# A two-block transformer forward pass on one core: the feed-forward's gated products are turned by VectorE in 32x32 blocks, where TensorE transposed them

## The chip, the cores and the metric

The kernel runs on 1 core of one Trainium2 chip. The metric is the device time of one execution in microseconds; lower is better.

## The reference, cut to what matters

256 tokens, model width 1024, float32. The first block has two layers, each with a feed-forward, a mixer (a latent attention in the first layer, a forget-gate attention in the second), a second feed-forward and a gated embedding; a second block with a pooling branch and a dilated attention follows. There are four feed-forwards of this form, with D_FF = 2816:

```
def swiglu(x, w_in, w_out):
    gate, up = jnp.split(x @ w_in, 2, axis=-1)
    return (jax.nn.silu(gate) * up) @ w_out

h = h + FFN_HALF * swiglu(rms_norm(h, g_ffn1[i]), ffn1_w_in[i], ffn1_w_out[i])
```

## The kernel before, in words

Each engine has a hand-written program, and semaphores order them. Every float32 product is made of three products of rounded parts: a matrix is split into a high part (a rounded copy, float32r) and a low part (the remainder), and hi x hi, hi x lo and lo x hi are added up in PSUM.

**Weights.** They come in groups of 128 x 2048 values. A group has a slot in each of three rings of four: `raw` (filled by SP's DMA queue, two transfers), `wh` (ScalarE's rounded copy, `split` at L1455 to L1461) and `wl` (VectorE's difference, `split` at L1983 to L1988). ScalarE's split of group g waits until TensorE has used group g-4 (`w_used`), TensorE waits for VectorE's part (`lo_done`), and SP may load raw again when VectorE's part is done (`room`, L439).

**A feed-forward** (`ffn` in each engine's program; f0 to f3) has two phases, with 33 groups of weights in all.

In the first phase there are 11 chunks (FCH) of 256 columns of gate and 256 of up. Each takes two groups (k = 0, 1), and TensorE makes 24 products of 128 x 512 for each: `tall_group`, L614 to L616. The result, for two tiles of 128 tokens, lies in one of two accumulators, by turns. ScalarE makes silu of the gate half (`silus`, L1544, into `sg`), and VectorE multiplies it with the up half (`gated`, L2140, into `a_n`, tokens on partitions). The second phase needs these products with features on partitions. So TensorE transposes them: four transposes of 128 x 128 for each chunk into a PSUM bank `M[c % 2]` (`turn_products`, L768 to L778; every transpose of the kernel is recorded at L690). They are placed between the two groups of the next chunk. ScalarE rounds the bank into `ah` (`round_a`, L1550), and VectorE writes the remainder into `al` (`rest_a`, L2147).

In the second phase there are 11 groups of `w_out` (L647 to L651; the first by `wide_first`), one for each chunk: TensorE multiplies `ah` and `al` of chunk c with the group and adds up all eleven. The eleventh chunk is transposed after the first of these groups. Before each group TensorE waits for the chunk's remainder (`m_read`).

In both phases ScalarE and VectorE split one or two groups ahead of TensorE. Their order for a chunk is: split, round or remainder of the chunk before, split, silu or gated product. On TensorE, ScalarE, VectorE and SP the middle chunks are a loop (`Fori`), the first one or three written out.

In f0 TensorE also makes a small bias table in three parts (L814, at chunks 2, 4 and 6 of the second phase), and VectorE copies it to `tsb` (L2178) after all its remainders. ScalarE stores `tsb` with a DMA (L1586) after the next norm. In f1 and f3 a tile `p_n` is transposed after the first group of the second phase, rounded to `ph` and its remainder written to `pl`.

Of the kernel before, what the change touches and what calls it, by code (L numbers as in the profile page):

```python
# [18 lines left out]
F32 = mybir.dt.float32  # L19
# [7 lines left out]
P = 128  # L27
# [49 lines left out]
def plan():  # L77


    sizes = {  # L80
        "norm": (0, 0, (1, 1, 1, 1), (4, 4, 4, 4)),
        "ffn": (33, 13, (6, 5, 0, 0), (6, 5, 0, 0)),
        "ffn_t": (33, 13, (6, 5, 0, G3), (6, 5, 0, G3)),
        "ffn_p": (33, 13, (6, 5, 1, 0), (6, 5, 1, 0)),
        "mla": (14, 12 + H, (H // 2 + 2, H // 2 + 2, H + 2, H + 1), (H + 2, H + 2, H + 2, H + 1)),
        "fox": (17, 9, (H, H, H, H + 3), (H, H, H, H + 3)),
        "ple": (5, 4, (0, 0, 0, 0), (0, 0, 0, 0)),
        "b2": (40, 26, tuple([n + 2 * (b == 3) for b, n in enumerate(U_FILLS)]),
               tuple([n + 2 * (b == 3) for b, n in enumerate(U_FILLS)])),
    }  # L90
    order = [("n0", "norm"), ("f0", "ffn_t"), ("n1", "norm"), ("mla", "mla"), ("n2", "norm"),
             ("f1", "ffn_p"), ("n3", "norm"), ("p0", "ple"), ("n4", "norm"), ("f2", "ffn"), ("n5", "norm"),
             ("fox", "fox"), ("n6", "norm"), ("f3", "ffn_p"), ("n7", "norm"), ("p1", "ple"), ("n8", "norm"),
             ("b2", "b2")]
    g = q = 0
    f, r = [0] * 4, [0] * 4
    at = {}
    for name, kind in order:
        at[name] = (g, q, tuple(f), tuple(r))
        dg, dq, df, dr = sizes[kind]  # L100
        g, q = g + dg, q + dq
        f = [a + b for a, b in zip(f, df)]
        r = [a + b for a, b in zip(r, dr)]
    return at, g


PLAN, NGROUPS = plan()


def heads_at():  # L110
# [40 lines left out]
def build(nc, I, out):  # L151
    with ExitStack() as ctx:
# [58 lines left out]
        x = region()  # L211
        ah = x("ah", [P, 2 * FCH, S], F32R)
        al = x("al", [P, 2 * FCH, S], F32R)
        sg = x("sg", [P, 2, NT, 256])
        a_n = x("a_n", [P, 2, NT, 256])
        p_n = x("p_n", [P, NT, PLE])
        ph = x("ph", [P, 2, S], F32R)
        pl = x("pl", [P, 2, S], F32R)
# [15 lines left out]
        kpe = x("kpe", [P, NT, ROPE])  # L234
        kpr = x("kpr", [P, NT, ROPE])
        x = region()
        x("below", [P, 1], offset=2 * (2 * FCH * S * 4) + 2 * (2 * NT * 256 * 4) - 32)
        causal_f = x("causal_f", [P, P])
        onehot = x("onehot", [33, TAB])
        rb = x("rb", [33, NH2])  # L240
        tsb = x("tsb", [H8, TAB])
        hraw = x("hraw", [P, 4])
        rgain = x("rgain", [P, 2, ROPE])
        freq = x("freq", [P, 16])
# [97 lines left out]
        rstd_done = sem("rstd_done")  # L342
        xh_done = sem("xh_done")
        silu_done = sem("silu_done")
        ah_done = sem("ah_done")
        gate_done = sem("gate_done")
        lat_sq = sem("lat_sq")
        lat_rstd = sem("lat_rstd")
# [240 lines left out]
        def _(pe):  # L589
# [164 lines left out]
            def ffn(name, nname, r, after, r_after, with_p=None):  # L754
# [3 lines left out]
                def chunk(c, i=0):  # L758

                    q, g = q0 + c, g0 + 2 * c  # L760
                    open_acc(q, i)
                    for k in range(2):
                        wait_group(g + k, i)
                        tall_group(g + k, q, xh, xl, 4 * k, 4, 512, k == 0, k == 1)
                        if k == 0:
                            turn_products(c - 1, i)

                def turn_products(c, i=0):  # L768

                    b, q = c % 2, q0 + c  # L770
                    pe.wait_ge(acc_read[q % 2], acc_reads(q) + 2 * i)
                    if r0[b] + c // 2 > 0:
                        pe.wait_ge(m_read[b], r0[b] + c // 2 + i)
                    for t in range(NT):
                        for k in range(2):
                            mm = turn(b, slice(k * S + t * P, k * S + (t + 1) * P),
                                      a_n[:, b, t, k * P:(k + 1) * P])
                    mm.then_inc(m_ready[b], 1)  # L778

                peel = 3 if g0 == 0 else 1  # L780
                first_fill(nname, r, g0, q0)
# [5 lines left out]
                q, g = q0 + FCH, g0 + 2 * FCH  # L787
                for c in range(FCH):
                    wait_group(g + c)
                    pe.wait_ge(m_read[c % 2], r0[c % 2] + c // 2 + 1)  # L790
                    if c == 0:
                        wide_first(g, q, ah, al)
                    else:
# [1 line left out]
                            wide_tile(g + c, q, t, ah, al, 2 * c, False, c == FCH - 1,  # L795
                                      turn_h(after, r_after) if t and c == FCH - 1 else None)
                    if c == 0:
                        turn_products(FCH - 1)
                        if with_p is not None:
                            open_m(2, r0[2])  # L800
                            pe.wait_ge(p_in, 16 * (with_p + 1))
                            for t in range(NT):
                                for k in range(2):
                                    mm = turn(2, slice(k * S + t * P, k * S + (t + 1) * P),
                                              p_n[:, t, k * P:(k + 1) * P])
                            mm.then_inc(m_ready[2], 1)
# [632 lines left out]
        def _(act):  # L1439
# [95 lines left out]
            def ffn(name, r):  # L1535
# [11 lines left out]
                def round_a(c, i=0):  # L1547
                    b = c % 2
                    act.wait_ge(m_ready[b], f0[b] + c // 2 + 1 + i)
                    act.activation(ah[:, bass.ds(i * 4 + 2 * c, 2), :],  # L1550
                                   M[:, b, :].rearrange("p (k n) -> p k n", k=2), ACT.Copy).then_inc(ah_done, 1)

                peel = 3 if g0 == 0 else 1
                for c in range(peel):
                    split_to(g0 + 2 * c + 3)
                    if c:
                        round_a(c - 1)
                    split_to(g0 + 2 * c + 4)
                    silus(c)
                    if g0 == 0 and c == 1:  # L1560

                        act.wait_ge(angles, 1)
                        act.activation(cs[:, :, :, :], rc[:, :, :, :], ACT.Sin).then_inc(sines, 1)
                with act.Fori(0, (FCH - peel) // 2) as i:
                    for c in range(peel, peel + 2):
                        split(g0 + 2 * c + 2, i)
                        round_a(c - 1, i)
                        split(g0 + 2 * c + 3, i)
                        silus(c, i)
                done[0] = g0 + 2 * FCH + 2  # L1570
                split_to(g0 + 2 * FCH + 3)
                round_a(FCH - 1)
# [393 lines left out]
        def _(dve):  # L1966
# [164 lines left out]
            def ffn(name, r, after):  # L2131

                g0, q0, f0, _ = PLAN[name]
                base = FIRST_SILU[name] * FCH

                def gated(c, i=0):
                    q = q0 + c
                    for t in range(NT):
                        dve.wait_ge(silu_done, NT * (base + c) + t + 1 + 4 * i)
                        dve.scalar_tensor_tensor(a_n[:, c % 2, t, :], acc(q, t)[:, 256:512], rstd[:, t:t + 1],  # L2140
                                                 sg[:, c % 2, t, :], ALU.mult, ALU.mult)\
                           .then_inc(acc_read[q % 2], 1)

                def rest_a(c, i=0):
                    b = c % 2
                    dve.wait_ge(ah_done, base + c + 1 + 2 * i)
                    dve.tensor_tensor(al[:, bass.ds(i * 4 + 2 * c, 2), :], pair(M[:, b, :]),  # L2147
                                      ah[:, bass.ds(i * 4 + 2 * c, 2), :].bitcast(F32), ALU.subtract)\
                       .then_inc(m_read[b], 1)

                peel = 3 if g0 == 0 else 1
                for c in range(peel):
                    split_to(g0 + 2 * c + 3)
                    if c:
                        rest_a(c - 1)
                    split_to(g0 + 2 * c + 4)
                    gated(c)
                    if g0 == 0:
                        (angles_reduced, head_constants, rope_tables)[c]()
                with dve.Fori(0, (FCH - peel) // 2) as i:  # L2160
                    for c in range(peel, peel + 2):
                        split(g0 + 2 * c + 2, i)
                        rest_a(c - 1, i)
                        split(g0 + 2 * c + 3, i)
                        gated(c, i)
                done[0] = g0 + 2 * FCH + 2
                split_to(g0 + 2 * FCH + 3)
                rest_a(FCH - 1)
# [4 lines left out]
                if g0 == 0:  # L2173
                    for j, c in enumerate(TABLE_AT):
                        split_to(g0 + 2 * FCH + c + 3)
                        dve.wait_ge(m_ready[3], f0[3] + j + 1)
                        w = 256 if j == 2 else 448
                        dve.tensor_copy(tsb[:, 448 * j:448 * j + w], M[0:H8, 3, 0:w]).then_inc(m_read[3], 1)  # L2178
# [838 lines left out]
```

## Time and profile before

| | |
|---|---|
| runs | 1335.22, 1335.80, 1337.46 us; median 1335.8 |
| profiled execution | 1334.0 us from the first to the last instruction (the only time recorded of it), 17481 instructions |
| granted TensorE clock, mean | 0.999 |
| TensorE products, busy | 1316.9 us (99%) |
| TensorE weight loads, busy | 1078.6 us (81%) |
| VectorE busy | 798.0 us (60%), 1036 instructions |
| ScalarE busy | 679.8 us (51%) |
| GpSimd busy | 129.9 us (10%) |
| DMA | 236.46 MB, mean 177 GB/s |

Busy time of TensorE counts products that overlap once, so a stretch that is busy throughout says that it never ran dry, and not at what pace it worked; the pace is in the starts of its instructions. The feed-forwards lie at about 15 to 197, 314 to 501, 532 to 718 and 842 to 1030 us.

### The profile page before, as it was taken

The page shows a single profiled execution, that of the slowest core. Times are in us where ns is not written, and L with a number is a line of the kernel's source. Part 1 is how long each engine was busy: PE and PEld are TensorE (multiplying, and loading weights), DVE is VectorE, ACT ScalarE, POOL GpSimd, SP SyncE. Part 2 cuts the span into 40 slices and gives each one's busy share as a digit, 9 for nine tenths or more (in the row PEclk, how much of TensorE's full clock was granted, in tenths as well). Part 3 has the DMA queues.
Part 4 walks back from the last instruction along what each step waited for, and adds up shares of the span by engine and source line. Part 5 has one row for each costly group of instructions (what it writes and reads, how often), then busy time and mean ns, then how long its engine had stood idle before and what let it go on. Part 6 is the DMA issues. An engine that isn't in the chain of part 4 may idle for free.

```text
span 1334.0 us, 17481 instructions
## 1 busy us (share of the span) xinstructions
PE 1316.9 (99%) x6474; PEld 1078.6 (81%) x6474; DVE 798.0 (60%) x1036; ACT 679.8 (51%) x959; POOL 129.9 (10%) x199
## 2 busy tenths in 40 slices
PE   9999999999999999999999999999999999999997
PEld 6888788788888887888888777888888887788886
DVE  6755448885555546655544667655554655665674
ACT  7444427755444426644444557544443646457542
POOL 2000002712000000000000330100000042110000
PEclk9999999999999999999999999999999999999999
DMA  9665544236655654555563654455564397555441
GB/s 301 217 189 189 189 154 167 96 98 188 203 181 185 220 193 146 179 185 184 182 208 127 223 188 127 135 189 184 186 217 169 127 284 230 168 162 172 160 158 32
DMA packets 148782, 236.46 MB, mean 177 GB/s; under 512 B 10087, under 2 KB 103447, under 8 KB 148208
## 3 DMA queue, kind: packets, MB, share of 16 engines
q1 hardware_dynamic: 143600, 222.26, 51.3%
q0 software_dynamic: 4736, 12.96, 3.2%
q8 instruction: 40, 0.66, 0.2%
q10 hardware_dynamic: 384, 0.41, 0.1%
q14 instruction: 22, 0.18, 0.0%
HBM read 233.43 MB, written 4.51 MB: 178 GB/s over the span
## 4 chain that ended last, share of the span: by engine, by line
PE 89%; DVE 5%; ACT 3%; issue 2%; DMA 0%; POOL 0%; SPq 0%; POOLq 0%; DVEq 0%; ACTq 0%
PE acc L614 20%; PE acc L616 19%; PE acc L615 19%; PE acc L647 7%; PE acc L648 7%; PE acc L651 7%; PE misc L690 5%; DVE wl L1987 1%; ACT wh L1461 1%; PE misc L1270 1%; PE misc L1127 1%; DMA raw<-in_ffn_w_in_dram 0%; ACT xh L1505 0%; DVE pT L2325 0%; DVE wl L1995 0%
## 5 line engine op out<-in xcount | busy, mean ns | idle before, releaser
L1987 DVE TENSOR_TENSOR wl<-raw,wh 128x2048 fp32r<-128x2048 f32 (+2 forms) x201 | 453.2, 2261 | 263.1 <-ACT wh L1461 262.9
L1461 ACT ACTIVATE wh<-raw 128x2048 fp32r<-128x2048 f32 (+2 forms) x207 | 388.9, 1889 | 137.3 <-PE acc L651 124.6
L614 PE MATMUL acc<-wh,xh 128*128 128x512 f32 (+1 forms) x832 | 328.9, 395 | 1.8 <-DVE xl L2031 0.8
L616 PE MATMUL acc<-wh,xl 128*128 128x512 f32 (+1 forms) x832 | 323.2, 388 | 0.0
L615 PE MATMUL acc<-wl,xh 128*128 128x512 f32 (+1 forms) x832 | 322.6, 388 | 0.0
L614 PEld LDWEIGHTS acc<-wh,xh 128*128 128x128 f32 x832 | 156.3, 188 | 35.9 <-DVE wl L1980 3.4
L616 PEld LDWEIGHTS acc<-wh,xl 128*128 128x128 f32 x832 | 156.2, 188 | 32.8
L615 PEld LDWEIGHTS acc<-wl,xh 128*128 128x128 f32 x832 | 156.4, 188 | 30.1
L647 PE MATMUL acc<-wh,ah 128*128 128x512 f32 x320 | 125.6, 393 | 0.0
L648 PE MATMUL acc<-wl,ah 128*128 128x512 f32 x320 | 124.6, 389 | 0.0
L614 PE MATMUL acc<-wh,zh 128*128 128x512 f32 x272 | 108.5, 399 | 0.5 <-DVE zl L2031 0.5
L616 PE MATMUL acc<-wh,zl 128*128 128x512 f32 x272 | 106.2, 390 | 0.0
L615 PE MATMUL acc<-wl,zh 128*128 128x512 f32 x272 | 106.0, 390 | 0.0
L1550 ACT ACTIVATE ah<-misc 128x512 f32 (+1 forms) x44 | 26.4, 600 | 155.9 <-PE misc L690 155.9
L2809 POOL TENSOR_SCALAR rstd<-ssq 128x1 f32<-128x1 f32 x19 | 10.4, 548 | 919.5 <-ACT hn L1493 919.3
L651 PE MATMUL acc<-wh,al 128*128 128x512 f32 x320 | 98.6, 389 | 0.0
L1544 ACT ACTIVATE sg<-acc,rstd 128x256 f32<-128x256 f32 x88 | 41.4, 475 | 100.5 <-PE acc L616 100.5
L2147 DVE TENSOR_TENSOR al<-misc,ah 128x512 f32 (+1 forms) x44 | 30.4, 692 | 84.0 <-ACT ah L1550 83.9
L1505 ACT ACTIVATE xh<-misc,gains 128x128 fp32r<-128x128 f32 x128 | 40.5, 365 | 69.2 <-PE misc L690 60.2
L647 PEld LDWEIGHTS acc<-wh,ah 128*128 128x128 f32 x320 | 60.1, 188 | 13.8 <-issue 1.7
L651 PEld LDWEIGHTS acc<-wh,al 128*128 128x128 f32 x320 | 60.1, 188 | 12.7
L648 PEld LDWEIGHTS acc<-wl,ah 128*128 128x128 f32 x320 | 60.1, 188 | 12.2
(363 smaller groups left out, 1655.9 us busy)
## 6 DMA issues: line engine op xcount, KB each, us to landing
raw<-in_ffn_w_in_dram SPq DMA_DIRECT2D x172, 512.0 KB, 4.7
raw<-in_ffn_w_out_dram SPq DMA_DIRECT2D x88, 512.0 KB, 4.4
raw<-in_w_in_dram SPq DMA_DIRECT2D x64, 512.0 KB, 4.9
raw<-in_fox_w_in_dram SPq DMA_DIRECT2D x24, 512.0 KB, 4.4
raw<-in_ple_w_gate_dram SPq DMA_DIRECT2D x16, 512.0 KB, 4.1
raw<-in_mla_w_o_dram SPq DMA_DIRECT2D x8, 512.0 KB, 4.0
raw<-in_fox_w_o_dram SPq DMA_DIRECT2D x8, 512.0 KB, 4.6
raw<-in_w_out_dram SPq DMA_DIRECT2D x8, 512.0 KB, 4.3
```

The lines of the kernel that those rows point to most:

```text
L614: pe.matmul(dst, hi, rhs_h, start=first, stop=False)
L615: pe.matmul(dst, hi, rhs_l, start=False, stop=False)
L616: return pe.matmul(dst, lo, rhs_h, start=False, stop=last)
L647: pe.matmul(acc(q + n, t), xa, wh[:, s, r], start=st, stop=False)
L648: pe.matmul(acc(q + n, t), xa, wl[:, s, r], start=False, stop=False)
L651: mm = pe.matmul(acc(q + n, t), xb, wh[:, s, r], start=False, stop=en)
L690: return pe.transpose(M[0:rows, b, cols], src, m[:, :])
L1461: act.activation(wh[:, s, 0:n], raw[:, s, 0:n], ACT.Copy).then_inc(hi_done, 1)
L1505: act.activation(x_cols(xh, r, k, t), turned(r, k, t), ACT.Copy, scale=gains[:, c:c + 1]).then_inc(xh_done, 1)
L1544: act.activation(sg[:, c % 2, t, :], acc(q, t)[:, 0:256], ACT.Silu, scale=rstd[:, t:t + 1]).then_inc(silu_done, 1)
L1987: dve.tensor_tensor(wl[:, s, 0:n], raw[:, s, 0:n], wh[:, s, 0:n].bitcast(F32), ALU.subtract)\
L2147: dve.tensor_tensor(al[:, bass.ds(i * 4 + 2 * c, 2), :], pair(M[:, b, :]), ah[:, bass.ds(i * 4 + 2 * c, 2), :].bitcast(F32), ALU.subtract)\
```

## The change

VectorE turns the gated products itself. Its transpose instruction turns 32 x 32 blocks within a quarter of the partitions; a full turn of 128 x 128 is put together from 16 pairs (source quarter i, target quarter o). One instruction takes one such pair for three chunks (the last time two) and both token tiles, so 32 partitions by 384 (256) elements. `a_n` is now wide enough for two batches of three chunks. The turned products `aT` lie in SBUF, in the place of `al`, and the remainder is written over them. The 16 instructions of a batch are dealt out over later iterations by `BATCH_PART`: batch 0 (chunks 0 to 2) over iterations 3 to 5, batch 1 over 6 to 8, batch 2 over 9 to 11, batch 3 (two chunks) over 12 to 15, where 11 to 15 are groups 0 to 4 of the second phase. Rounding and remainder of chunks 0 and 1 are at chunks 9 and 10, those of chunk c+2 at group c of the second phase. TensorE loses `turn_products` and waits for `al_done`. ScalarE's and VectorE's loops are written out; `tsb` moves into the place of `a_n`, its three copies come between the remainders, and VectorE waits for its store (`table_out`) in the attention stage.

```
+QUAD = 32
+BATCHES = ((0, 3), (3, 6), (6, 9), (9, 11))
+BATCH_PART = {3: (0, 0, 5), 4: (0, 5, 10), 5: (0, 10, 16), 6: (1, 0, 5), 7: (1, 5, 10), 8: (1, 10, 16),
+              9: (2, 0, 5), 10: (2, 5, 10), 11: (2, 10, 16), 12: (3, 0, 4), 13: (3, 4, 8), 14: (3, 8, 12), 15: (3, 12, 16)}
+EARLY_A = 2
...
+        aT = x("aT", [P, 2 * FCH, S], offset=2 * FCH * S * 4)
         sg = x("sg", [P, 2, NT, 256])
-        a_n = x("a_n", [P, 2, NT, 256])
+        a_n = x("a_n", [P, 2, NT, 768])
...
-        tsb = x("tsb", [H8, TAB])
+        tsb = x("tsb", [H8, TAB], offset=2 * (2 * FCH * S * 4) + 2 * NT * 256 * 4)
...
                         tall_group(g + k, q, xh, xl, 4 * k, 4, 512, k == 0, k == 1)
-                        if k == 0:
-                            turn_products(c - 1, i)
-
-                def turn_products(c, i=0):
...
-                    for t in range(NT):
-                        for k in range(2):
-                            mm = turn(b, slice(k * S + t * P, k * S + (t + 1) * P),
-                                      a_n[:, b, t, k * P:(k + 1) * P])
-                    mm.then_inc(m_ready[b], 1)
...
                     wait_group(g + c)
-                    pe.wait_ge(m_read[c % 2], r0[c % 2] + c // 2 + 1)
+                    pe.wait_ge(al_done, FIRST_SILU[name] * FCH + c + 1)
...
-                        turn_products(FCH - 1)
...
+                def round_a(c):
+
+                    batch = [n for n, (a, b) in enumerate(BATCHES) if a <= c < b][0]
+                    act.wait_ge(turned_done, len(BATCHES) * FIRST_SILU[name] + batch + 1)
+                    act.activation(ah[:, 2 * c:2 * c + 2, :], aT[:, 2 * c:2 * c + 2, :], ACT.Copy).then_inc(ah_done, 1)
+
+                for c in range(FCH):
                     split_to(g0 + 2 * c + 3)
-                    if c:
-                        round_a(c - 1)
+                    if c >= FCH - EARLY_A:
+                        round_a(c - FCH + EARLY_A)
                     split_to(g0 + 2 * c + 4)
                     silus(c)
...
+                for c in range(FCH - EARLY_A):
+                    split_to(g0 + 2 * FCH + c + 3)
+                    round_a(c + EARLY_A)
...
+                        w = slice(256 * (c % 3), 256 * (c % 3) + 256)
+                        dve.scalar_tensor_tensor(a_n[:, (c // 3) % 2, t, w], acc(q, t)[:, 256:512], rstd[:, t:t + 1],
                                                  sg[:, c % 2, t, :], ALU.mult, ALU.mult)\
                            .then_inc(acc_read[q % 2], 1)
...
+                def turned_blocks(n):
+
+                    batch, first, last = BATCH_PART[n]
+                    a, b = BATCHES[batch]
+                    if first == 0:
+                        dve.wait_ge(acc_read[(q0 + b - 1) % 2], acc_reads(q0 + b - 1))
+                    for m in range(first, last):
+                        i, o = m % 4, m // 4
+                        src = a_n[QUAD * i:QUAD * i + QUAD, batch % 2, :, 0:256 * (b - a)]
+                        dst = aT[QUAD * o:QUAD * o + QUAD, 2 * a:2 * b, :]
+                        e = dve.transpose(dst.rearrange("p c (t i r) -> p t c i r", t=NT, i=4)[:, :, :, i, :],
+                                          src.rearrange("p t (c o r) -> p t c o r", o=4, r=QUAD)[:, :, :, o, :])
+                    if last == 16:
+                        e.then_inc(turned_done, 1)
+
+                def rest_a(c):
+                    dve.wait_ge(ah_done, base + c + 1)
+                    dve.tensor_tensor(al[:, 2 * c:2 * c + 2, :], aT[:, 2 * c:2 * c + 2, :],
+                                      ah[:, 2 * c:2 * c + 2, :].bitcast(F32), ALU.subtract).then_inc(al_done, 1)
+
+                for c in range(FCH):
                     split_to(g0 + 2 * c + 3)
+                    if c >= FCH - EARLY_A:
+                        rest_a(c - FCH + EARLY_A)
+                    if c in BATCH_PART:
+                        turned_blocks(c)
                     split_to(g0 + 2 * c + 4)
                     gated(c)
...
+                for c in range(FCH - EARLY_A):
+                    split_to(g0 + 2 * FCH + c + 3)
+                    if FCH + c in BATCH_PART:
+                        turned_blocks(FCH + c)
+                    rest_a(c + EARLY_A)
+                    if g0 == 0 and c in TABLE_AT:
+                        table(TABLE_AT.index(c))
...
             split_to(g + 5)
+            dve.wait_ge(table_out, 16)
             rest_latents(range(4, 6))
```

## Rows read from the trace of the kernel before

**Rows 1.** The page: busy us (share of the span) and instructions.
```profile
PE 1316.9 (99%) x6474; PEld 1078.6 (81%) x6474; DVE 798.0 (60%) x1036; ACT 679.8 (51%) x959; POOL 129.9 (10%) x199
```

**Rows 2.** The page: chain that ended last, by engine and by line.
```profile
PE 89%; DVE 5%; ACT 3%; issue 2%; DMA 0%; POOL 0%; SPq 0%; POOLq 0%; DVEq 0%; ACTq 0%
PE acc L614 20%; PE acc L616 19%; PE acc L615 19%; PE acc L647 7%; PE acc L648 7%; PE acc L651 7%; PE misc L690 5%; DVE wl L1987 1%; ACT wh L1461 1%; PE misc L1270 1%; PE misc L1127 1%; DMA raw<-in_ffn_w_in_dram 0%; ACT xh L1505 0%; DVE pT L2325 0%; DVE wl L1995 0%
```

**Rows 3.** Stretches: length; busy us of PE, PEld, DVE, ACT, POOL; clock; DMA share; GB/s.
```profile
20.00:142.00 122.00, 121.78 (x558) 100.45 (x557) 75.70 (x99) 59.66 (x60) 2.56 (x4) 1.00 0.65 206
...
540.00:655.00 115.00, 115.00 (x528) 95.14 (x527) 65.83 (x57) 55.88 (x59) 2.06 (x2) 1.00 0.59 185
```

**Rows 4.** Waits of the whole span: total us, times, longest.
```profile
DVE wl L1987 <- ACT wh L1461: 262.9, 154, 6.1
ACT ah L1550 <- PE misc L690: 155.9, 44, 3.7
...
DVE al L2147 <- ACT ah L1550: 83.9, 42, 2.1
...
DVE tsb L2178 <- PE misc L814: 18.4, 3, 7.0
```

**Rows 5.** Timeline, TensorE, third feed-forward: start, us, line, operands, count.
```profile
551.00 0.60 PE L690 MATMUL misc<-ident,a_n 128*128 128x128 f32 x4
...
664.63 0.60 PE L690 MATMUL misc<-ident,a_n 128*128 128x128 f32 x4
```

**Rows 6.** Timeline, ScalarE, second phase of the third feed-forward; in brackets idle time.
```profile
676.26 1.92 ACT L1461 ACTIVATE wh<-raw 128x2048 fp32r<-128x2048 f32 x1 [3.52 <-PE acc L651]
...
687.14 1.92 ACT L1461 ACTIVATE wh<-raw 128x2048 fp32r<-128x2048 f32 x1 [3.52 <-PE acc L651]
```

**Rows 7.** Timeline, TensorE, around one group of transposes.
```profile
627.60 0.39 PE L616 MATMUL acc<-wh,xl 128*128 128x512 f32 x1
...
630.55 0.60 PE L690 MATMUL misc<-ident,a_n 128*128 128x128 f32 x4
630.90 0.48 PE L614 MATMUL acc<-wh,xh 128*128 128x512 f32 x1
631.22 0.39 PE L615 MATMUL acc<-wl,xh 128*128 128x512 f32 x1
```

**Rows 8.** Groups by form: count, busy us, mean ns, idle us before.
```profile
L690 PE MATMUL misc<-ident,a_n 128*128 128x128 f32 x176 | 26.3, 271 | 0.0
```

**Rows 9.** VectorE by line: ns min/median/max, first and last start; last row as rows 8.
```profile
L2325 DVE COPY pT<-misc x16: 542/544/558, 255.1 to 291.5; 128x384 f32<-128x384 f32 x16
...
L1995 DVE TENSOR_TENSOR wl<-raw,wh x12: 676/678/685, 270.8 to 294.5; 128x512 fp32r<-128x512 f32 x12
...
L2178 DVE COPY tsb<-misc x3: 410/611/611, 152.9 to 176.5; 8x448 f32<-8x448 f32 x2, 8x256 f32<-8x256 f32 x1
...
L1987 DVE TENSOR_TENSOR wl<-raw,wh 128x2048 fp32r<-128x2048 f32 x194 | 443.2, 2291 | 256.7 <-ACT wh L1461 256.5
```

**Rows 10.** Timeline, VectorE, two neighbours without a wait.
```profile
223.13 0.48 DVE L433 TENSOR_SCALAR kn<-acc,lrs 128x256 f32<-128x256 f32 x1
223.52 0.48 DVE L433 TENSOR_SCALAR vn<-acc,lrs 128x256 f32<-128x256 f32 x1
```

**Rows 11.** Timeline, VectorE, first phase of the third feed-forward.
```profile
625.82 0.48 DVE L2140 SCALAR_TENSOR_TENSOR a_n<-acc,rstd,sg 128x256 f32<-128x256 f32 x1 [0.20 <-ACT sg L1544]
627.62 2.29 DVE L1987 TENSOR_TENSOR wl<-raw,wh 128x2048 fp32r<-128x2048 f32 x1 [1.32 <-ACT wh L1461]
```

**Rows 12.** Timeline, ScalarE, the same stretch.
```profile
625.68 1.91 ACT L1461 ACTIVATE wh<-raw 128x2048 fp32r<-128x2048 f32 x1
```

**Rows 13.** ScalarE, copies of 128x512 from SBUF.
```profile
L1453 ACT ACTIVATE wh<-raw x8: 620/634/652, 5.5 to 13.1; 128x512 fp32r<-128x512 f32 x8
```

**Rows 14.** Timeline of ScalarE's queue and VectorE: the table's store, the first write there.
```profile
204.91 0.55 ACTq L1586 DMA_DIRECT2D bias_table<-tsb  x1
...
217.69 0.87 DVE L2205 SCALAR_TENSOR_TENSOR ll<-misc,gains,lh 128x256 fp32r<-128x256 f32 x2
```

More of the change, by code:

```diff
@@ L81, in plan @@
         "norm": (0, 0, (1, 1, 1, 1), (4, 4, 4, 4)),
-        "ffn": (33, 13, (6, 5, 0, 0), (6, 5, 0, 0)),
-        "ffn_t": (33, 13, (6, 5, 0, G3), (6, 5, 0, G3)),
-        "ffn_p": (33, 13, (6, 5, 1, 0), (6, 5, 1, 0)),
+        "ffn": (33, 13, (0, 0, 0, 0), (0, 0, 0, 0)),
+        "ffn_t": (33, 13, (0, 0, 0, G3), (0, 0, 0, G3)),
+        "ffn_p": (33, 13, (0, 0, 1, 0), (0, 0, 1, 0)),
         "mla": (14, 12 + H, (H // 2 + 2, H // 2 + 2, H + 2, H + 1), (H + 2, H + 2, H + 2, H + 1)),
@@ L236, in build @@
         x = region()
-        x("below", [P, 1], offset=2 * (2 * FCH * S * 4) + 2 * (2 * NT * 256 * 4) - 32)
+        x("below", [P, 1], offset=2 * (2 * FCH * S * 4) + 2 * NT * 256 * 4 + 2 * NT * 768 * 4 - 32)
         causal_f = x("causal_f", [P, P])
@@ L344, in build @@
         silu_done = sem("silu_done")
+        turned_done = sem("turned_done")
         ah_done = sem("ah_done")
+        al_done = sem("al_done")
         gate_done = sem("gate_done")
@@ L764, in chunk @@
                         tall_group(g + k, q, xh, xl, 4 * k, 4, 512, k == 0, k == 1)
-                        if k == 0:
-                            turn_products(c - 1, i)
-                def turn_products(c, i=0):
[L770 to L773, printed above, removed]
-                    for t in range(NT):
-                        for k in range(2):
-                            mm = turn(b, slice(k * S + t * P, k * S + (t + 1) * P),
-                                      a_n[:, b, t, k * P:(k + 1) * P])
-                    mm.then_inc(m_ready[b], 1)
                 peel = 3 if g0 == 0 else 1
@@ L1545, in silus @@
                                        scale=rstd[:, t:t + 1]).then_inc(silu_done, 1)
[L1547 to L1554, printed above, removed]
+                def round_a(c):
[3 more added lines that the diff above has]
+                for c in range(FCH):
                     split_to(g0 + 2 * c + 3)
-                    if c:
-                        round_a(c - 1)
+                    if c >= FCH - EARLY_A:
+                        round_a(c - FCH + EARLY_A)
                     split_to(g0 + 2 * c + 4)
@@ L1563, in ffn @@
                         act.activation(cs[:, :, :, :], rc[:, :, :, :], ACT.Sin).then_inc(sines, 1)
[L1564 to L1572, printed above, removed]
+                for c in range(FCH - EARLY_A):
+                    split_to(g0 + 2 * FCH + c + 3)
+                    round_a(c + EARLY_A)
                 if name in ("f1", "f3"):
@@ L2134, in ffn, with table @@
                 base = FIRST_SILU[name] * FCH
+                def table(j):
+                    dve.wait_ge(m_ready[3], f0[3] + j + 1)
+                    w = 256 if j == 2 else 448
+                    dve.tensor_copy(tsb[:, 448 * j:448 * j + w], M[0:H8, 3, 0:w]).then_inc(m_read[3], 1)
                 def gated(c, i=0):
@@ L2139, in gated @@
                         dve.wait_ge(silu_done, NT * (base + c) + t + 1 + 4 * i)
-                        dve.scalar_tensor_tensor(a_n[:, c % 2, t, :], acc(q, t)[:, 256:512], rstd[:, t:t + 1],
+                        w = slice(256 * (c % 3), 256 * (c % 3) + 256)
+                        dve.scalar_tensor_tensor(a_n[:, (c // 3) % 2, t, w], acc(q, t)[:, 256:512], rstd[:, t:t + 1],
                                                  sg[:, c % 2, t, :], ALU.mult, ALU.mult)\
                            .then_inc(acc_read[q % 2], 1)
[L2144 to L2149, printed above, removed]
@@ L2151, in ffn @@
-                peel = 3 if g0 == 0 else 1
-                for c in range(peel):
+                def turned_blocks(n):
[11 more added lines that the diff above has]
+                        e.then_inc(turned_done, 1)
@@ L2153, in ffn @@
+                def rest_a(c):
[3 more added lines that the diff above has]
+                for c in range(FCH):
                     split_to(g0 + 2 * c + 3)
-                    if c:
-                        rest_a(c - 1)
+                    if c >= FCH - EARLY_A:
+                        rest_a(c - FCH + EARLY_A)
+                    if c in BATCH_PART:
+                        turned_blocks(c)
@@ L2156, in ffn @@
                     split_to(g0 + 2 * c + 4)
                     gated(c)
-                    if g0 == 0:
+                    if g0 == 0 and c < 3:
                         (angles_reduced, head_constants, rope_tables)[c]()
[L2160 to L2165, printed above, removed]
@@ L2166, in ffn @@
-                done[0] = g0 + 2 * FCH + 2
-                split_to(g0 + 2 * FCH + 3)
-                rest_a(FCH - 1)
+                for c in range(FCH - EARLY_A):
[5 more added lines that the diff above has]
+                        table(TABLE_AT.index(c))
                 if name in ("f1", "f3"):
@@ L2172, in ffn @@
                        .then_inc(m_read[2], 1)
[L2173 to L2178, printed above, removed]
                 split_to(g0 + 3 * FCH + 2)
```

## The prediction

> **What bounds the kernel now.** I read the page's busy times first, then the chain, then the waits, then single chunks. TensorE is busy in 1316.9 of 1334.0 us, VectorE in 798.0, ScalarE in 679.8 [rows 1]. The chain that ended last is 89% TensorE, and the line that records every transpose has 5% of it [rows 2]. In a long stretch of each feed-forward TensorE has no idle time: 115.00 busy of 115.00 us in the third one, at a granted clock of 1.00, with VectorE at 65.8 and the DMA engines at 0.59 [rows 3]. The first has 121.78 of 122.00 us, and the other two are like the third. The waits say who follows whom: ScalarE waits for TensorE (155.9 us for the transposes alone), VectorE waits for ScalarE (262.9 us for the high parts of weights, 83.9 us for those of products), and no wait of TensorE for either of them stands in the rows of a feed-forward [rows 4]. So a feed-forward lasts as long as the instructions TensorE is given, while the others keep up.
>
> **What is removed from TensorE.** Each of 44 chunks has a group of four transposes. One group begins at 551.00 us and the one ten chunks on at 664.63 [rows 5]: 11.363 us a chunk. Without transposes the pace can be read in the second phase, where ScalarE's splits follow TensorE directly: one starts at 676.26 and the second behind it at 687.14, so 5.44 us for a group of 24 products [rows 6], and 10.88 us for the 48 of a chunk. The difference, 0.483 us, is what four transposes take with what they disturb. The single rows say the same: the transposes begin at 630.55, the next product at 630.90 and the one behind it at 631.22, which is 0.35 us and then 0.32 in place of 0.23, together 0.44; the other 0.04 is in slightly longer steps of the next few products [rows 7]. All 44 groups lie in stretches without idle time, the eleventh of each feed-forward behind the first wide group too. The sum is 44 x 0.483 = 21.3 us. The lower bound is the 0.44 of the single rows: 44 x 0.44 = 19.4 us. TensorE now waits for al_done where it waited for m_read: one wait for another, and all products are queued behind it. Its price is nothing while the low parts come early, which is the rest of the working.
>
> A transpose has a mean duration of 271 ns [rows 8], and 176 of them would be 47.7 us. These durations overlap: the row with four of them shows 0.60 us of busy time, and the next product starts after 0.35 [rows 7]. The sum goes by starts. The Trainium skill (TensorE: Matmul & The Clock Gate, Part 4: PE-mode transpose) gives about 275 ns for a transpose in a kernel's context, which agrees with the duration in this row; priced so, the change would bring 176 x 0.275 = 48 us. The same sum from the row is rival D.
>
> **What is added to VectorE.** Per feed-forward 48 turns of 32 x 384 elements and 16 of 32 x 256, 256 in all. No row shows a 32x32 turn, nor a tile moved from one quarter of the partitions to another. The nearest by form is a copy of 384 elements a partition: 544 ns [rows 9]. The rows of 512 and 2048 elements (678 and 2291 ns) give 1.05 ns an element and 0.14 us fixed, so 0.54 us for 384; a copy on 8 partitions takes no less for being narrow (448 elements, 611 ns) [rows 9]. I take 0.55 us for the large turns and 0.42 for the small ones. The lower end is 0.46, if starts overlap by 0.09 as two neighbours do in the rows (start to start 0.39 where each takes 0.48) [rows 10]. For the upper end I let every 4-byte element take four steps: 384 x 4 x 1.05 ns + 0.14 = 1.75 us. I take the lower value since every VectorE row of this trace moves one 4-byte element in about 1.05 ns. The Trainium skill (Vector Engine (DVE) Microarchitecture Reference, 3.8) says that the turning front end sustains one element per cycle per lane; no run here shows that yet, and by it the turn would cost as the copy.
>
> **Can VectorE carry it?** First phase, per chunk of 10.88 us: two splits of 2.29 and two gated products of 0.48 [rows 11] are 5.54, and five or six turns add 3.3: 8.8 of 10.88. In the order of the code: the gated products of one chunk end at 626.3, the split behind them starts at 627.62 because ScalarE's starts at 625.68 after its silus [rows 11, 12] and ends at 629.9. Six turns end at 633.2, the second split at 635.5. The next silus come 10.88 us behind the last pair, at about 635.5. So the gated products hardly move. What TensorE needs is later: the group split at 629.9 is used from about 636.2 on, and the one split at 635.5 from 641.6. The margin is 6 us, and 10 us for the gated products, since their accumulator is wanted two chunks on. Behind the turns only those two are queued. The raw slot is given back to SP's queue up to 3.3 us later, and the next split of that slot is 20 us off.
>
> Second phase, per group of 5.44 us: a split (2.29), a remainder of products (0.68, the 128x512 row from SBUF), and six large turns in the first group (3.3: 6.3 us) or four small ones in the next four (1.7: 4.7 us) [rows 9]. Only the first is over, by 0.9 us. VectorE's split for group c+2 can begin 1.95 us after TensorE starts group c-1 [rows 6], and the group is wanted three groups (16.3 us) after that start, so 10 us are left for the 6.3. The rounding of products moves to the last two chunks and the second phase: ScalarE then has 1.92 + 0.63 us in 5.44 [rows 6, 13]. Each rounding waits for turns that ended three or more iterations before; behind it only the next split is queued.
>
> At the first feed-forward the three copies of the bias table now come between remainders. VectorE already waits there for TensorE's small product [rows 4]; when released it has 4.7 us of work, and TensorE holds two finished groups (10.9 us). The new wait for table_out in the attention stage is covered: the DMA is issued at 204.91 and VectorE gets to that place at 217.69 [rows 14]. Two engines get straight code for a loop, and neither has the chain in a feed-forward. I cost all of this at nothing, and up to 0.5 us for each feed-forward (2 us in all) at the other end.
>
> **The sum.** 1334.0 - 21.3 = 1312.7 us for the profiled span. The median of the runs lies 1.8 us above that span, and I keep this: 1335.8 - 21.3 = 1314.5 us. With the bounds (19.4 to 21.3 gained, 0 to 2 given back) and 1.5 us for the spread of runs, the forecast's own range is 1313 to 1320.
>
> **Rivals.**
> A: slower, because VectorE becomes the bound. Its work from chunk 3 to group 4 of the second phase is 8 x 5.54 + 5 x 2.97 + 2 x 0.68 = 60.5 us, plus 48 large and 16 small turns. TensorE has 8 x 10.88 + 6 x 5.44 = 119.7 us until it wants the last result. At 0.55 and 0.42 us the work is 94 us. At T us for a large and 0.67T + 0.05 for a small one it passes 119.7 at T = 0.99, and the whole gain of 5.3 us for each feed-forward is lost at 1.08. From there on the kernel is slower. At 1.75 us the work is 164 us, TensorE waits 44 us in each feed-forward, and the time is 1314.5 + 178 = 1492 us. For it: no row shows a turn. Against it: the pace of all other rows [rows 9]; even two steps an element (0.95 us) would pass.
> B: no change that can be told. Either T lies near 1.05, or a hand-over that I cost at nothing (turns, rounding, remainder, wait for al_done) takes back 4 to 5 us of each feed-forward, say at its border, where six turns coincide with the first wide group: 1335. Against it are margins of 6 us and more in each place.
> C: two thirds of the gain. VectorE and ScalarE read SBUF where they read PSUM, and TensorE's products slow down. One per cent of the 0.227 us step over the 792 products (33 x 24) of each of four feed-forwards would be 7 us: 1321.7. Against it: from 627.60 to 630.55 TensorE takes 13 steps of 0.227 us, with VectorE's split beside most of them (627.62 to 629.9), and the mean step of the second phase, where VectorE idles over half of the time, is 5.44 / 24 = 0.227 too [rows 6, 7, 11].
> D: the transposes cost their duration, 48 us: 1288. Against it are the starts [rows 7] and the two paces [rows 5, 6].
>
> **How the numbers follow.** Forecast 0.84, A 0.07, B 0.03, C 0.04, D 0.02. The time is the forecast's, 1314.5. The range 1311 to 1322 holds it with C and leaves out A, B and D. Differences below 0.2% (2.7 us) can't be told from none. Faster: 0.84 + 0.04 + 0.02 = 0.90; within: 0.03; slower: 0.07.
>
> **What would show it.** Right: a chunk period of 10.88 us in the first phase, no transposes of a_n, turns of 0.5 to 0.6 us, VectorE's busy time up by about 256 x 0.5 = 130 us to some 925, ScalarE's hardly changed, TensorE without idle time in the four stretches. Wrong: waits of TensorE for VectorE's wl or al lines inside a feed-forward, turns above 1 us, or a step of products other than 0.227 us.

## The result, and the profile after

The changed kernel takes 1314.34 us (median of 4 runs, 1314.08 to 1314.75) against 1335.74 before: ratio 0.9839, 95% interval 0.9828 to 0.9851. The forecast was 1314.5. The profiled span went from 1334.0 to 1312.5 us.

The page after gives busy time by engine (as rows 1), the chain by line (as rows 2) and the turns as a group:

```profile
PE 1294.6 (99%) x6298; PEld 1060.6 (81%) x6298; DVE 929.2 (71%) x1292; ACT 675.6 (51%) x959; POOL 129.7 (10%) x199
...
PE acc L623 20%; PE acc L625 20%; PE acc L624 20%; PE acc L656 7%; PE acc L657 7%; PE acc L660 7%; PE misc L699 4%; DVE wl L1974 1%; ACT wh L1455 1%; PE misc L1264 1%; PE misc L1121 1%; DMA raw<-in_ffn_w_in_dram 0%; ACT xh L1499 0%; DVE pT L2326 0%; DVE wl L1982 0%
...
L2148 DVE STREAM_TRANSPOSE aT<-a_n 32x384 f32<-32x384 f32 (+1 forms) x256 | 137.2, 536 | 3.9
```

VectorE works 131.2 us more than in [rows 1] and TensorE 22.3 less. The span, 21.5 us shorter, follows TensorE. A stretch of the third feed-forward is still without idle time of TensorE (as rows 3):

```profile
535.00:645.00 110.00, 110.00 (x487) 91.09 (x486) 82.13 (x87) 48.37 (x46) 0.00 (x0) 1.00 0.64 202
```

The waits of the whole span (as rows 4). The 155.9 us that ScalarE spent waiting for transposes are gone, and it waits for the products themselves, 242.0 us where it was 100.5. The first row is of the kernel before, the others are of the changed one:

```profile
ACT sg L1544 <- PE acc L616: 100.5, 80, 2.4
...
ACT sg L1538 <- PE acc L625: 242.0, 80, 6.1
DVE wl L1974 <- ACT wh L1455: 178.8, 99, 6.1
...
DVE a_n L2134 <- ACT sg L1538: 49.9, 76, 3.9
...
DVE tsb L2127 <- PE misc L808: 6.4, 2, 5.4
```

The first phase on VectorE's timeline (as rows 11; the second row of gated products of each chunk is left out). The gated products start 10.88 us apart, the forecast period. Before them VectorE idles 0.87 to 1.00 us behind five turns and 0.25 behind six; where a chunk has five turns and a remainder it is 0.26 to 0.40:

```profile
600.05 0.48 DVE L2134 SCALAR_TENSOR_TENSOR a_n<-acc,rstd,sg 128x256 f32<-128x256 f32 x1 [1.00 <-ACT sg L1538]
...
613.41 2.29 DVE L1974 TENSOR_TENSOR wl<-raw,wh 128x2048 fp32r<-128x2048 f32 x1 [1.32 <-ACT wh L1455]
615.74 3.50 DVE L2148 STREAM_TRANSPOSE aT<-a_n 32x384 f32<-32x384 f32 x6
619.26 2.29 DVE L1974 TENSOR_TENSOR wl<-raw,wh 128x2048 fp32r<-128x2048 f32 x1
621.81 0.48 DVE L2134 SCALAR_TENSOR_TENSOR a_n<-acc,rstd,sg 128x256 f32<-128x256 f32 x1 [0.25 <-ACT sg L1538]
```

The border between the phases is the narrow place. Here are ScalarE's last silu and the split behind it, then VectorE, and then the first product of the third group (index 2) on TensorE:

```profile
643.74 0.47 ACT L1538 ACTIVATE sg<-acc,rstd 128x256 f32<-128x256 f32 x1 [0.20 <-PE acc L625]
644.11 1.91 ACT L1455 ACTIVATE wh<-raw 128x2048 fp32r<-128x2048 f32 x1
...
646.05 2.29 DVE L1974 TENSOR_TENSOR wl<-raw,wh 128x2048 fp32r<-128x2048 f32 x1 [1.32 <-ACT wh L1455]
648.38 3.50 DVE L2148 STREAM_TRANSPOSE aT<-a_n 32x384 f32<-32x384 f32 x6
651.90 0.69 DVE L2155 TENSOR_TENSOR al<-aT,ah 128x512 fp32r<-128x512 f32 x1
...
654.42 0.39 PE L656 MATMUL acc<-wh,ah 128*128 128x512 f32 x1
```

The remainder of chunk 2 ends at 652.59 and is wanted at 654.42, so 1.8 us are left.

### The profile page after: what moved, and what is told of

It reads as the page before. It is cut to its first block, busy times and chain, and to the rows that moved or that the text cites. A ratio compares the mean times of both kernels' runs of the same rounds, so it can differ in the third digit from the quotient of the medians.

```text
span 1312.5 us, 16855 instructions
## 1 busy us (share of the span) xinstructions
PE 1294.6 (99%) x6298; PEld 1060.6 (81%) x6298; DVE 929.2 (71%) x1292; ACT 675.6 (51%) x959; POOL 129.7 (10%) x199
## 4 chain that ended last, share of the span: by engine, by line
PE 89%; DVE 5%; ACT 3%; issue 2%; DMA 0%; POOL 0%; SPq 0%; POOLq 0%; DVEq 0%; ACTq 0%
PE acc L623 20%; PE acc L625 20%; PE acc L624 20%; PE acc L656 7%; PE acc L657 7%; PE acc L660 7%; PE misc L699 4%; DVE wl L1974 1%; ACT wh L1455 1%; PE misc L1264 1%; PE misc L1121 1%; DMA raw<-in_ffn_w_in_dram 0%; ACT xh L1499 0%; DVE pT L2326 0%; DVE wl L1982 0%
## 5 line engine op out<-in xcount | busy, mean ns | idle before, releaser
L623 PE MATMUL acc<-wh,xh 128*128 128x512 f32 (+1 forms) x832 | 325.0, 391 | 2.4 <-DVE xl L2018 1.4
L1538 ACT ACTIVATE sg<-acc,rstd 128x256 f32<-128x256 f32 x88 | 41.4, 475 | 242.1 <-PE acc L625 242.0
L2148 DVE STREAM_TRANSPOSE aT<-a_n 32x384 f32<-32x384 f32 (+1 forms) x256 | 137.2, 536 | 3.9
L2134 DVE SCALAR_TENSOR_TENSOR a_n<-acc,rstd,sg 128x256 f32<-128x256 f32 x88 | 42.0, 483 | 49.9 <-ACT sg L1538 49.9
```

The lines of the kernel that those rows point to most:

```text
L623: pe.matmul(dst, hi, rhs_h, start=first, stop=False)
L2134: dve.scalar_tensor_tensor(a_n[:, (c // 3) % 2, t, w], acc(q, t)[:, 256:512], rstd[:, t:t + 1], sg[:, c % 2, t, :], ALU.mult, ALU.mult)\
L2148: e = dve.transpose(dst.rearrange("p c (t i r) -> p t c i r", t=NT, i=4)[:, :, :, i, :], src.rearrange("p t (c o r) -> p t c o r", o=4, r= ...
```

## Experiments

**What do transposes cost TensorE?** Three kernels. The first is the changed kernel with four transposes of a constant tile put back at each of the 44 places. Their result is not used, and VectorE's turns stay:

```
+                        if k == 0:
+                            idle_turns(c - 1, i)
...
+                def idle_turns(c, i=0):
...
+                    pe.wait_ge(acc_read[q % 2], acc_reads(q) + 2 * i)
+                    for n in range(4):
+                        turn(b, slice(n * P, (n + 1) * P), ident[:, :])
...
+                        idle_turns(FCH - 1)
```

> The changed kernel, with four transposes of a constant tile put back on TensorE at each of the 44 old places (the result is not used; VectorE's turns stay). Theory (the gain is the TensorE time of the transposes and nothing else): 44 x 0.44 to 0.483 us come back, 1333.7 to 1335.6 us. Rival (the gain came from the shorter chain of hand-overs through PSUM and ScalarE, and TensorE's transposes filled gaps): it stays at 1314 to 1316 us. Rival (the transposes cost their duration, 271 ns): 1314.3 + 47.7 = 1362 us.

Measured: 1336.03 us, ratio to before 1.0003 (0.9994 to 1.0013). The whole gain is given back, with VectorE's turns and the shorter path through SBUF still in place. So the gain is TensorE's time, and the rival that speaks of hand-overs falls.

The second and third are the kernel before, with each transpose issued twice (eight in place of four), and with `k in range(1)` in place of `range(2)`. The last leaves two of the four transposes out, so half of each turned tile is stale.

> The kernel before, with each of the four transposes of a chunk issued twice (8 for each chunk). Theory (a transpose costs TensorE its start-to-start time): the chain of before has 0.44 us for 4 and 0.87 to 0.89 for 8, so 44 x 0.44 = 19.4 us more, 1355.1 us. Rival (it costs its duration of 271 ns): 47.7 us more, 1383 us. Rival (the cost is the break in the stream of products, not the transposes): less than 5 us more.

> The kernel before, with two of the four transposes of a chunk left out (half of each turned tile is stale). Theory: 88 transposes fewer at 0.109 us, 9.6 us less: 1326.1 us. Rival (the break is the cost): under 3 us less, 1333 us. Together with 0, 4 and 8 transposes this gives a fixed cost for each break and a cost for each transpose.

Measured: 1354.71 us with 8 (ratio 1.0142, 1.0126 to 1.0157) and 1325.59 with 2 (0.9925, 0.9909 to 0.9940). With 0, 2, 4 and 8 transposes for each of 44 breaks in the stream of products the times are 1314.34, 1325.59, 1335.7 and 1354.71; the first of the four is the changed kernel, the others are the kernel before and its two variants. A transpose so costs 0.108 us (from 4 to 8) to 0.115 (from 2 to 4), and two of them with their break cost 0.256 (from 0 to 2), which leaves some 0.03 to 0.04 us for the break. Neither the duration nor the break is the price. The timeline of the kernel with 8 shows it:

```profile
621.38 1.03 PE L690 MATMUL misc<-ident,a_n 128*128 128x128 f32 x8
622.17 0.48 PE L614 MATMUL acc<-wh,xh 128*128 128x512 f32 x1
```

Eight transposes take 0.79 us from start to start, where four took 0.35 [rows 7].

**How much more could VectorE take?** Turns were issued once more, into the place of `ah` that ScalarE overwrites later, for every second turn (x1.5) or each (x2). In the kernel x3 the turns of the first three batches are issued a third time, into a spare tile. The edit of x1.5 (in x2 it holds for every m):

```
+                        if m % 2:
+                            dst = aU[QUAD * o:QUAD * o + QUAD, 2 * a:2 * b, :]
+                            e = dve.transpose(...)
```

> Every second turn of VectorE is issued twice (the second result goes to a place that is overwritten later). From the trace after, a large turn takes 0.58 us from start to start and a small one 0.445. Theory of the threshold: VectorE's work from chunk 3 to group 4 is 60.5 + 72 x 0.58 + 24 x 0.445 = 113 us, below the 119.7 that TensorE has: no change, 1314.3 us (to 1316). Rival (VectorE's added time is paid as soon as a chunk's order is disturbed): part of the 17.5 us added for each feed-forward, up to 70 us in all, 1320 to 1384 us.

> Every turn is issued twice. Theory of the threshold: 60.5 + 96 x 0.58 + 32 x 0.445 = 130.4 us against 119.7, so 10.7 us for each feed-forward, 43 in all: 1357 us. Rival (margin is larger than reckoned, by the groups split ahead): 1314 to 1335 us. Rival (all added time is paid): 1314.3 + 4 x 35 = 1454 us.

> Every turn of the first three batches is issued three times, those of the last batch twice. Theory of the threshold: 60.5 + 144 x 0.58 + 32 x 0.445 = 158.3 us against 119.7, so 38.6 us for each feed-forward, 154 in all: 1469 us. Between this run and the one with all turns twice the slope should be one to one: 48 x 0.58 x 4 = 111 us more. Rival (another bound catches it, for instance ScalarE's order): a slope other than one to one.

Measured: 1314.48 us (ratio 0.984, 0.9823 to 0.9856), 1331.26 (0.9967, 0.9955 to 0.998) and 1417.16 (1.0612, 1.0594 to 1.063). Half as many turns again cost nothing that can be told, twice as many cost 17 us, and three times 103. There is a threshold, and it lies between 1.5 and 2. The sizes expected above it were too high, 43 and 154. One reason stands in VectorE's timeline of the kernel with x2:

```profile
94.77 0.57 DVE L2149 STREAM_TRANSPOSE aT<-a_n 32x384 f32<-32x384 f32 x1
95.27 0.53 DVE L2153 STREAM_TRANSPOSE aU<-a_n 32x384 f32<-32x384 f32 x1
95.81 0.57 DVE L2149 STREAM_TRANSPOSE aT<-a_n 32x384 f32<-32x384 f32 x1
```

Two turns with the same source and target quarters take 1.04 us, not 2 x 0.58: the second starts 0.50 us after the first. With 1.04 and 0.77 us for a pair, the formula of rival A gives 60.5 + 48 x 1.04 + 16 x 0.77 = 122.7 us against 119.7, 3.0 us for each feed-forward and 1326 us in all. In the x3 kernel three turns take 1.50 us (from 89.97 to 91.47), which gives 144.8 us and 1415. Both are within 5 us of what was measured, from below. In the x2 kernel the rest is no lower clock. A stretch of its first feed-forward, in which TensorE already waits:

```profile
100.00:140.00 40.00, 38.50 (x170) 31.54 (x170) 39.64 (x56) 19.80 (x19) 0.00 (x0) 1.00 0.59 198
```

The granted clock is 1.00, as in the other stretches read of the first and third feed-forward, and VectorE is busy for 39.64 of 40.00 us. The 0.36 us between its instructions come to about 1 us in the 120 of a feed-forward (an estimate from this row), where 1.2 us are missing; that they are the same time is not shown. From x2 to x3 the time grows by 85.9 us for 192 more turns of 0.46 us, 88 us: one to one, as expected of an engine that is the bound.

**One burst, and chunk by chunk.** Two other ways of dealing out the same work:

```
-BATCH_PART = {3: (0, 0, 5), 4: (0, 5, 10), 5: (0, 10, 16), ...
+BATCH_PART = {5: (0, 0, 16), 8: (1, 0, 16), 11: (2, 0, 16), 15: (3, 0, 16)}
```

> The 16 turns of a batch stand in one iteration (5, 8, 11 and 15) instead of being dealt out over three or four. Theory: the second split of that iteration ends 3.6 + 16 x 0.58 + 2.3 = 15.2 us after the gated products before it, and TensorE wants it at 15.3: no margin left, 0 to 1 us lost for each feed-forward, 1314 to 1318 us. Rival (margins are smaller than reckoned): each of the large bursts costs some 3 us, 1314 + 4 x 3 x 3 = 1350 us. Rival (dealing out matters not at all): 1314.3 within 0.5.

Measured: 1340.46 us (ratio 1.003, 1.002 to 1.0041). With the same 256 turns the kernel is 26 us slower than the changed one and no better than before. It was not the split, for which the expectation had reckoned the margin. TensorE waits four times for the remainder `al`, once in each feed-forward:

```profile
PE acc L655 <- DVE al L2154: 14.5, 4, 3.9
```

The place is the border. VectorE there, then the product that waits for it:

```profile
133.24 2.29 DVE L1973 TENSOR_TENSOR wl<-raw,wh 128x2048 fp32r<-128x2048 f32 x1 [1.32 <-ACT wh L1454]
135.44 9.31 DVE L2147 STREAM_TRANSPOSE aT<-a_n 32x384 f32<-32x384 f32 x16
144.79 0.69 DVE L2154 TENSOR_TENSOR al<-aT,ah 128x512 fp32r<-128x512 f32 x1
...
145.63 0.47 PE L655 MATMUL acc<-wh,ah 128*128 128x512 f32 x1 [3.86 <-DVE al L2154]
```

The four waits are 14.5 of the 24.7 us that the span grew by. More comes behind them, in TensorE's clock (stretches as rows 3; the clock is the third value from the right; the last row is the stretch behind the wait of the third feed-forward):

```profile
141.00:145.60 4.60, 0.77 (x4) 0.31 (x3) 4.49 (x9) 2.43 (x2) 0.00 (x0) 1.00 0.00 0
145.60:150.00 4.40, 4.37 (x13) 3.49 (x14) 4.40 (x3) 0.00 (x0) 0.00 (x0) 0.66 0.28 65
150.00:155.00 5.00, 5.00 (x19) 3.21 (x19) 2.21 (x4) 1.91 (x2) 0.00 (x0) 0.96 0.97 349
...
671.00:675.40 4.40, 4.33 (x10) 3.47 (x11) 4.40 (x3) 0.00 (x0) 0.00 (x0) 0.50 0.31 64
```

After TensorE has idled for 3.9 us the granted clock averages 0.66 over 4.4 us, a mix of the two levels, 1.2 and 2.4 GHz, and products start 0.43 us apart in place of 0.227 from 147.15 to 150.14. The 14 products from 145.63 to 150.50 take 4.87 us, not 3.18: this wait costs 1.7 us more than itself. The other three, of 3.4 to 3.9 us, are followed by 1.6 to 2.5 us of lost pace, 7.5 us for all four. With the waits that is 22.0 of the 24.7 us; the rest I did not place.

To test that this one remainder is the cause, it was moved away from behind the burst. The roundings and remainders of chunks 0 to 2 each come one iteration earlier, and VectorE also waits for its own third batch before the table's copies:

```
-EARLY_A = 2
+EARLY_A = 3
...
+                    dve.wait_ge(turned_done, 3)
```

> The burst kernel (16 turns of a batch in one iteration), with rounding and remainder of chunks 0 to 2 one iteration earlier (EARLY_A = 3), so that no remainder that is wanted at group 2 stands behind the burst of iteration 11. (VectorE also waits for its own third batch before the table's copies, which it has passed by then.) Theory (the 26 us of the burst are one late remainder for each feed-forward, al of chunk 2, and the lower clock behind that wait): 1314 to 1317 us. Rival (a burst is too much for the splits or the accumulator too): 1325 to 1340 us.

Measured: 1320.36 us (ratio 0.9885, 0.987 to 0.99). 20 of the 26 us come back. No wait for `al` is left. The waits of TensorE's weight loads show what goes with the other 6 us, splits that stand behind bursts. In the changed kernel the first of these rows has 1.3 us and the second is not there:

```profile
PEld acc L622 <- DVE wl L1973: 6.6, 10, 1.0
...
PEld acc L655 <- DVE wl L1973: 2.6, 4, 1.0
```

Part of such a wait lies beside the product before it, so the sum of 9.2 us is more than what the span loses. Four of the places are in the first phases, one for each feed-forward. This is the one of the third, VectorE first and then TensorE:

```profile
618.53 0.69 DVE L2155 TENSOR_TENSOR al<-aT,ah 128x512 fp32r<-128x512 f32 x1
619.13 9.31 DVE L2148 STREAM_TRANSPOSE aT<-a_n 32x384 f32<-32x384 f32 x16
628.47 2.29 DVE L1973 TENSOR_TENSOR wl<-raw,wh 128x2048 fp32r<-128x2048 f32 x1
...
630.82 0.50 PE L622 MATMUL acc<-wh,xh 128*128 128x512 f32 x1 [0.53 <-DVE wl L1973]
```

The edit itself put the remainder of 0.69 us ahead of this burst. Without it, in the burst kernel, TensorE's step at the same place is only 0.1 us over its pace. So the test changed two things: it freed the remainder, and it used up what the split behind the burst of iteration 8 had left. The theory was right for the larger part, and the time lies 3 us above its upper end.

The other way turns each chunk alone, in the next iteration (`BATCH_PART = {c + 1: (c, 0, 16) ...}`).

> Each chunk is turned alone in the next iteration, 16 turns of 32 x 128 elements, in place of three chunks at once. Theory: a turn of 128 elements takes 0.14 + 128 x 1.05 ns + 0.01 = 0.29 us, 4.6 us for a chunk; VectorE then works 5.54 + 4.6 = 10.2 of 10.88 us in the first phase and is just in time: 1314 to 1316 us with about 50 us of turns for each feed-forward (34 now). Rival (a turn has a larger fixed cost, as a fill of the 32 x 32 array, 0.45 us each): 12.7 of 10.88 us, 1314 + 4 x (9 x 1.9 - 6) = 1358 us.

Measured: 1319.71 us (ratio 0.9885, 0.987 to 0.9901), 5.4 above the changed kernel. That misses the expected 1314 to 1316 by 4 us, and the rival's 1358 by far. A turn of 128 elements takes 0.303 us (0.29 expected), and there are 704 of them, 213 us for 137. The TensorE timeline has no step longer than 0.25 us over its pace in the other feed-forwards; its four waits for a split, 0.6 to 1.5 us, are at 38 to 64 us, in the first. They make its steps 4.5 us longer, of the 5.3 that the span grew by. There VectorE also makes constants, as here between two chunks:

```profile
50.36 0.87 DVE L2133 SCALAR_TENSOR_TENSOR a_n<-acc,rstd,sg 128x256 f32<-128x256 f32 x2
51.15 3.31 DVE L2082 TENSOR_TENSOR tab<-rgain,cs 128x16 f32<-128x16 f32 x16
54.49 0.17 DVE L2084 COPY mxp<-posf 128x2 f32<-128x2 f32 x1
54.57 2.28 DVE L1973 TENSOR_TENSOR wl<-raw,wh 128x2048 fp32r<-128x2048 f32 x1
56.77 5.04 DVE L2147 STREAM_TRANSPOSE aT<-a_n 32x128 f32<-32x128 f32 x16
```

Turning every chunk three iterations later (`BATCH_PART = {c + 3: ...}`, with EARLY_A = 3) takes the turns away from the constants.

> Chunk by chunk as before, but each chunk turned three iterations after it is made (3 to 13 in place of 1 to 11) and EARLY_A = 3. Theory (the 5.4 us of the chunk-by-chunk kernel are waits in the first feed-forward alone, where turns of chunks 0 and 1 meet the constants that VectorE makes there): the waits at 37 to 64 us go, 1314 to 1316 us. Rival (704 turns at 0.303 us are too much for VectorE in general): 1319 to 1330 us. Rival (three groups of the second phase now have 8.3 of 5.4 us of work, more than the lead allows): up to 2 us for each feed-forward, 1322 us.

Measured: 1318.02 us (ratio 0.9867, 0.9852 to 0.9882). The waits at 38 to 64 us are gone, as the theory said. Three new ones stand in the second phase of the second, third and fourth feed-forward, before the sixth group (index 5). The first row is the wait of all three; then come VectorE in the third feed-forward and the product that waits there:

```profile
PE acc L655 <- DVE wl L1973: 2.5, 3, 1.2
...
665.01 5.04 DVE L2147 STREAM_TRANSPOSE aT<-a_n 32x128 f32<-32x128 f32 x16
670.08 0.69 DVE L2154 TENSOR_TENSOR al<-aT,ah 128x512 fp32r<-128x512 f32 x1
670.69 2.28 DVE L1973 TENSOR_TENSOR wl<-raw,wh 128x2048 fp32r<-128x2048 f32 x1
...
673.03 0.50 PE L655 MATMUL acc<-wh,ah 128*128 128x512 f32 x1 [1.17 <-DVE wl L1973]
```

That is the second rival: three iterations of 7.9 us in the place of 5.44 use up the lead, and the split behind them is late. The product starts 0.8 to 1.3 us late at each place, about half the rival's price.

So each half of the theory holds, and the sum does not: chunk by chunk VectorE has no margin to spare in either place.

**Further the same way.** The two tiles `p_n` are turned by VectorE too, in groups 5 to 8.

> The changed kernel, and the two tiles p_n (eight transposes in all, in the second and the fourth feed-forward) are turned by VectorE too, 16 turns of 32 x 128 for each, four of them in each of groups 5 to 8. Theory: two breaks of 0.485 us go from TensorE, VectorE has the room: 1313.4 us. Rival (a wait at the end of the feed-forward, where p_n's rounded parts come later): no change or up to 2 us more.

Measured: 1313.66 us (1313.13 to 1314.27; ratio 0.9834, 0.9821 to 0.9848). The median is 0.7 us below the changed kernel's, which ran on another occasion, and the spans differ by 1.2 (1311.3 against 1312.5). The sign and size fit the theory, but the two intervals overlap for the most part. That this version is faster than the changed kernel is not shown.

## Why the prediction was right, and where it was not

- **Transposes, 44 x 0.483 = 21.3 us.** Right, in size and in mechanism. Putting them back costs 21.7 us, and the medians differ by 21.4. That starts count and not durations is shown by the kernels with 8 and 2.
- **Turns of 0.55 and 0.42 us.** They take 0.569 and 0.436 (mean of each form), 0.58 and 0.445 from start to start. The copy of 384 elements [rows 9] was the right neighbour, 4% low. From 256 to 384 elements a turn grows by 0.133 us, 1.04 ns an element. The Trainium skill (Vector Engine (DVE) Microarchitecture Reference, 3.8) has one element per cycle per lane; these runs agree with it as far as a turn moves an element in the time that VectorE's other instructions take for one (1.05 ns [rows 9]).
- **The lower end with overlap, 0.46.** Not reached: in the changed kernel each turn starts 0.01 us after the end of the one before. Turns overlap only where their quarters are the same, as in the x2 kernel.
- **First phase, 8.8 of 10.88 us.** Right: the chunk with six turns has 9.0, and 0.25 us are left before the gated products, which keep their period.
- **Second phase, "10 us are left for the 6.3".** This step was wrong, though the time it gave (nothing lost) was right. Its own numbers give 16.3 - 1.95 = 14.4 us for the 6.3. And I let VectorE's split start 1.95 us after TensorE starts group c-1, which at the border is not what holds it. ScalarE's split there stands behind the silus of the last chunk, which wait for the products of the first phase; it starts at 644.11, and VectorE's follows at 646.05. TensorE began the first wide group at 654.42 - 2 x 5.44 = 643.54, and wants the remainder of chunk 2 10.9 us after that. The margin is 1.8 us, neither the 3.7 of my sentence nor the 6 and more that rival B holds against itself. In the changed kernel this costs nothing because the last batch but one has only six turns left there, and I had not reckoned that path: here the forecast had luck. With 16 turns in that place the kernel lost 26 us, 20 of which came back without this one delay.
- **Rival A's threshold, 1.08 us a turn.** At 1.04 us for a pair the time is 17 us above the changed kernel, and at 1.50 for three turns it is 103 above. From 17 us to the 21.4 at which the whole gain is lost, rival A's sum needs another 0.02 us a turn, so the point is near 1.06 (an estimate from these two runs): about as reckoned. The sum is low by 5 us for the x2 kernel, where the clock is 1.00, and by 2 for x3. In the x3 run the mean clock is 0.979, but TensorE waits for VectorE there, so whether the lower clock costs anything is not shown.
- **Rivals B and C.** With the transposes put back the time is the old one to 0.4 us, so the hand-overs and the reads from SBUF together took or gave nothing that can be told. TensorE's pace didn't change: 0.227 us a product (648.98 to 654.42 for 24), and ScalarE's rounding from SBUF takes 614 ns where it was 600 from PSUM.
- **f0's table and table_out at nothing.** Right. VectorE's wait at the table fell from 18.4 [rows 4] to 6.4 us, and no wait for the table's store stands in its rows.

## What to carry to other kernels

Where one engine is busy throughout, price what leaves it by starts, not by durations, and check the price against two paces, one with the operation and one without. What is put on a second engine is free up to a threshold, but find the threshold by deadlines: follow the engine's own order from the last thing it must wait for to each result that is wanted, at phase borders above all. Spreading the added work so that no result stands behind a burst was worth 26 us here, more than the change itself, and 20 of them hung on one remainder in each feed-forward.

## What the runs showed of the hardware

- A VectorE turn of 32 x 384 elements between quarters of the partitions costs 4% more than a 128 x 384 copy (569 and 546 ns). Turns in a row don't overlap when the quarter changes (0.58 us from start to start for 0.569 each); with the same two quarters the next one starts 0.07 us before the end of the first (0.50 for 0.57). The Trainium skill (VectorE: DVE Perf Modes, Two Vector instructions with no wait between them) says that an instruction whose input or output starts in another quarter than the last one's is held until the earlier ones have finished; the timelines of the x2 and x3 kernels agree.
- Four transposes of 128 x 128 in a stream of 512-column products take 0.35 us of TensorE from start to start and eight take 0.79, some 0.11 us each, where the duration of one is 271 ns [rows 8].
- Behind four waits of TensorE of 3.4 to 3.9 us (burst kernel) the mean granted clock of the next 4.4 us was 0.50 to 0.66, and the lost pace added 1.6 to 2.5 us to each wait. Behind the waits of 0.6 to 1.5 us in the chunk-by-chunk kernel it was 1.00 (stretches of 5 to 6 us from 38, 50, 56 and 64 us).
